# A decoder step on one core: the DRAM scratch of the second projection's right operands, with the column group ahead of the partition

## The reference

```
h = rms_norm(x, norm_g) @ w_in                      # 2048 x 8192
b_gate, c_gate, hx, z = split(h, 4)
u = c_gate * hx
conv = conv3_causal(prev_u, u)
y = (b_gate * conv * silu(z)) @ w_out               # 2048 x 2048
x = x + y
```

## Time and profile before

| what | value |
|---|---|
| median of 3 runs | 2429.08 us (2425.07 to 2432.25) |
| the profiled execution's own time | 2431.18 us |
| its span | 2429.4 us |
| PE busy | 2342.1 us (96%) |
| DVE busy | 1687.6 us (69%) |
| ACT busy | 1240.2 us (51%) |
| DMA | 571.01 MB in 383174 packets, mean 235 GB/s |
| queue q1 (SyncE), share of 16 DMA engines | 55.0% |
| queue q10 (ScalarE), share | 12.1% |
| PE L1085 and L1089 in the chain that ended last | 22% and 11% of the span |
| "DMA left<-in_w_out_a_dram" in the same chain | 2% |
| loads right_a_rounded<-y_right_scratch | x8, 952 KB, 11.1 us to landing |
| loads right_b_rounded<-y_right_scratch | x6, 952 KB, 14.4 us to landing |

### The profile page before, as it was taken

How to read it: one execution, slowest core, us unless ns; L and a number is a source line. 1 busy time by engine, 2 the same in 40 slices (tenths; PEclk the granted TensorE clock), 3 DMA queues, 4 the chain that set the end, 5 groups by cost and what they waited for, 6 DMA issues and landing times.

```text
span 2429.4 us, 49387 instructions
## 1 busy us (share of the span) xinstructions
PE 2342.1 (96%) x20006; PEld 2041.6 (84%) x20006; DVE 1687.6 (69%) x1984; ACT 1240.2 (51%) x2236; POOL 109.0 (4%) x69
## 2 busy tenths in 40 slices
PE   5999999999998999999999999999999989899998
PEld 4999999999998999999998999999999733355554
DVE  6888788878876884555898978787667667533311
ACT  5544444444443446777555477776655346421111
POOL 3000000000000111000000000000000022200000
PEclk9999999999998999999999999999999999999999
DMA  6243444344348666235577777887889899999998
GB/s 198 87 133 105 137 129 124 103 134 130 104 145 314 211 204 220 87 104 183 197 263 252 248 280 242 302 269 267 280 301 321 309 381 422 369 371 383 383 406 302
DMA packets 383174, 571.01 MB, mean 235 GB/s; under 512 B 19513, under 2 KB 304690, under 8 KB 363698
## 3 DMA queue, kind: packets, MB, share of 16 engines
q1 hardware_dynamic: 305858, 461.55, 55.0%
q10 hardware_dynamic: 76960, 106.03, 12.1%
q0 software_dynamic: 128, 0.26, 0.0%
HBM read 508.24 MB, written 59.54 MB: 234 GB/s over the span
## 4 chain that ended last, share of the span: by engine, by line
PE 82%; DVE 6%; DMA 5%; ACT 3%; issue 2%; SPq 0%; ACTq 0%; DVEq 0%
PE psum L1085 22%; PE psum L1738 18%; PE psum L1089 11%; PE psum L1746 8%; PE psum L2444 8%; PE psum L1789 4%; PE psum L2523 4%; DMA left<-in_w_out_a_dram 2%; PE psum L2502 1%; DVE h_keys_turned L1680 1%; PE psum L1754 1%; PE psum L2483 1%; DMA w_raw<-in_w_in_b_dram 1%; ACT w_raw L1501 1%; PE psum L1768 1%
## 5 line engine op out<-in xcount | busy, mean ns | idle before, releaser
L1738 PE MATMUL psum<-x_hi,w_hi 128*128 128x272 f32 x2048 | 434.4, 293 | 4.3 <-DVE x_lo L993 2.9
L1738 PE MATMUL psum<-x_lo,w_hi 128*128 128x272 f32 x2048 | 425.9, 289 | 0.0
L456 ACT ACTIVATE left_rounded<-left 128x1024 fp32r<-128x1024 f32 x280 | 295.1, 1055 | 192.0 <-PE psum L1089 174.5
L1085 PE MATMUL psum<-right_a_rounded,left_rounded 128*128 128x272 f32 x2560 | 352.3, 290 | 8.8 <-DVE right_a_rounded L779 4.6
L771 DVE TENSOR_TENSOR left_rounded<-left,left_rounded 128x1024 fp32r<-128x1024 f32 x280 | 345.5, 1237 | 20.8 <-ACT left_rounded L456 20.4
L1085 PEld LDWEIGHTS psum<-right_a_rounded,left_rounded 128*128 128x128 f32 x2560 | 335.2, 190 | 10.0 <-issue 8.2
L1738 PEld LDWEIGHTS psum<-x_hi,w_hi 128*128 128x128 f32 x2048 | 322.0, 189 | 21.6 <-issue 21.1
L1738 PEld LDWEIGHTS psum<-x_lo,w_hi 128*128 128x128 f32 x2048 | 322.1, 189 | 0.0
L1680 DVE STREAM_TRANSPOSE h_keys_turned<-h_ring 128x1024 f32<-128x1024 f32 x256 | 300.0, 1215 | 19.7 <-PE psum L1789 10.7
L1746 PE MATMUL psum<-x_hi,w_lo 128*128 128x272 f32 x2048 | 286.1, 295 | 0.0
L1746 PEld LDWEIGHTS psum<-x_hi,w_lo 128*128 128x128 f32 x2048 | 265.9, 189 | 8.5 <-issue 4.9
(11 more groups left out here) (253 smaller groups left out, 2738.0 us busy)
## 6 DMA issues: line engine op xcount, KB each, us to landing
h_ring<-in_cache_k_dram SPq DMA_DIRECT2D x256, 512.0 KB, 6.4
ring<-in_cache_v_dram SPq DMA_DIRECT2D x128, 1024.0 KB, 7.9
left<-in_w_in_a_dram SPq DMA_DIRECT2D x128, 512.0 KB, 4.0
w_raw<-in_w_kv_dram SPq DMA_DIRECT2D x16, 2048.0 KB, 12.8
w_raw<-in_w_in_b_dram SPq DMA_DIRECT2D x15, 2048.0 KB, 9.6
left<-in_w_out_a_dram SPq DMA_DIRECT2D x32, 512.0 KB, 5.8
wo_raw<-in_w_out_b_dram SPq DMA_DIRECT2D x32, 512.0 KB, 8.6
ring<-in_w_out_b_dram SPq DMA_DIRECT2D x16, 1024.0 KB, 7.3
```

Source lines behind the costliest of these rows:

```text
L456: act.activation(arena.left_high(q), arena.left(LEFT[mm], n), ACT.Copy).then_inc(hi_ready, 1)
L1085: pe.matmul(to, wh[:, k * P:(k + 1) * P], arena.right(RIGHT[mm], low)[:, k * GT:(k + 1) * GT], start=(mm in OPENS and k == 0 and low == 0) ...
L1738: pe.matmul(psum[n % 2][:, g, 0:GT], m.WH[n % 2][:, k * P:(k + 1) * P], x[:, k * T + g * GT:k * T + (g + 1) * GT], start=(k == 0 and x is ...
```

## The change

The scratch's dimensions are reordered from (piece, operand, partition, group, column) to (piece, operand, group, partition, column). Before, one partition of one operand was 8 groups of 1088 bytes behind each other in DRAM, and the load of the first seven groups read 7616 contiguous bytes for a partition. Now the 128 partitions of one group lie behind each other, and the load reads 7 rows of 1088 bytes for a partition. In the stores only the destination's addresses move: their rows were 1088 bytes, 8704 apart, and are 1088 bytes, 1088 apart, for the partitions of a group. No instruction is added, removed or moved on any engine; the 14 loads have another shape (128x7x272 instead of 128x1904), and the bytes are the same.

```diff
-                        act.dma_start(st.YS.rearrange("l e p i t -> l i p e t")[0, past][:, 0:3, :],
+                        act.dma_start(st.YS.rearrange("l e i p t -> l i p e t")[0, past][:, 0:3, :],
                                       quarters(low_high.bitcast(F32))).then_inc(y_out, 16)
...
                 for low in range(2):
-                    act.dma_start(arena.right(order, low)[:, 0:(EDGE - 1) * GT].bitcast(F32),
-                                  st.YS[low, entry].rearrange("p i t -> p (i t)")[:, 0:(EDGE - 1) * GT]).then_inc(right_in[mm], 16)
+                    act.dma_start(arena.right(order, low)[:, 0:(EDGE - 1) * GT].bitcast(F32).rearrange("p (i t) -> p i t", i=EDGE - 1),
+                                  st.YS[low, entry].rearrange("i p t -> p i t")[:, 0:EDGE - 1, :]).then_inc(right_in[mm], 16)
...
-        st.YS = nc.dram_tensor("y_right_scratch", (2, PRODUCTS, P, EDGE, GT), F32, kind="Internal").ap()
+        st.YS = nc.dram_tensor("y_right_scratch", (2, PRODUCTS, EDGE, P, GT), F32, kind="Internal").ap()
```

More of the change, by code:

```diff
@@ L543, in conv_extras @@
                         act.wait_ge(yh_ready, 2 * past + 2)
-                        act.dma_start(st.YS.rearrange("l e p i t -> l i p e t")[0, past][:, 0:3, :],
+                        act.dma_start(st.YS.rearrange("l e i p t -> l i p e t")[0, past][:, 0:3, :],
                                       quarters(low_high.bitcast(F32))).then_inc(y_out, 16)
-                        act.dma_start(st.YS.rearrange("l e p i t -> l i p e t")[0, past][:, 3:7, :],
+                        act.dma_start(st.YS.rearrange("l e i p t -> l i p e t")[0, past][:, 3:7, :],
                                       quarters(top_high.bitcast(F32))).then_inc(y_out, 16)
@@ L549, in conv_extras @@
                         act.wait_ge(yl_ready, 2 * past + 2)
-                        act.dma_start(st.YS.rearrange("l e p i t -> l i p e t")[1, past][:, 0, :], y4_low[:, 0, :]).then_inc(y_out, 16)
-                        act.dma_start(st.YS.rearrange("l e p i t -> l i p e t")[1, past][:, 1:3, :], y4_low[:, 2:4, :]).then_inc(y_out, 16)
-                        act.dma_start(st.YS.rearrange("l e p i t -> l i p e t")[1, past][:, 3:7, :], quarters(b1_rounded.bitcast(F32))).then_inc(y_out, 16)
+                        act.dma_start(st.YS.rearrange("l e i p t -> l i p e t")[1, past][:, 0, :], y4_low[:, 0, :]).then_inc(y_out, 16)
+                        act.dma_start(st.YS.rearrange("l e i p t -> l i p e t")[1, past][:, 1:3, :], y4_low[:, 2:4, :]).then_inc(y_out, 16)
+                        act.dma_start(st.YS.rearrange("l e i p t -> l i p e t")[1, past][:, 3:7, :], quarters(b1_rounded.bitcast(F32))).then_inc(y_out, 16)
                 if part == 2 and mm == 0:
```

## The result

The changed kernel takes 2438.92 us in the median of 20 runs (2435.29 to 2445.36), the kernel before 2431.11 us in the median of 20 on the same chips. The ratio is 1.0035, 95% interval 1.0028 to 1.0042: 7.8 us slower by the medians, 6.8 to 10.2 by the interval. The forecast was +4.9 us, and 2434.0 us for the median; 2.0 us of the distance to 2438.92 are the median of the kernel before, which was 2429.08 over the 3 runs known then. The profiled execution took 2438.66 us, its span 2436.8, against 2429.4.

The account below looks back on a forecast made before the run. PE, busy 96%, bounds the kernel, with 14.9 us lost in the loads' stretch. Step 33 later, +5.2, less 0.3 for its first product, gives +4.9: 2436.1 profiled, 2434.0 as median (runs' median 2.1 lower), range 2426 to 2441.

Parts of the forecast that it names:

- Turns between the queues: Load and weight queues alternate packets; with 1088-byte rows the weights' q1 gets near 35%, removing both waits for weights.
- The stores at nothing: The 35 stores keep row size and count, only addresses move; covered by over 10 us, priced at nothing.
- The loads' rows at 48 ns: A 1088-byte load row takes the store's 48 ns; the 14 loads' engine work rises from 32.5 to 37.6 us.
- Rival D: Reading 1088-byte rows costs more than writing them: +7.8 to about +11 us, taken as +9, 2438 us; chance 0.14.
- Rival C: 1088-byte rows move at the byte rate of 7616-byte rows, 41.4 ns each: +0.9 us, 2430.0 us; chance 0.07.
- ScalarE held at its issues: Load issues wait until about 1,230 rows are left ahead; last passes at 761.8, (32, 1) starts at 764.3 instead of 753.01.
- Rival B: ScalarE isn't held at the load issues; the DMA engines bound the stretch: -1.6 us, 2427.5 us; chance 0.18.
- What is won back: From (32, 1) on nothing is missing; six products take 18.1 us, step 33 starts at 782.4 instead of 777.19.
- I take nothing, the bound is +2.8: PE's clock after standing some 12 us inside (32, 0): a low clock priced at nothing, at most +2.8 us.
- slower by over 0.3%: Whole kernel over 7.3 us slower: chance 0.22, of it 0.14 dearer reads and 0.08 low clock or poor overlap.
- main case: ScalarE held at the load issues makes the kernel +4.9 us, 2434.0 us, bounds +2.6 to +9.1; chance 0.52.
- within 0.3%: Whole kernel's time within 7.3 us of no change: chance 0.71.

Follow-up runs that it names:

- stores_only: Changed kernel with loads reading 7616 contiguous bytes per partition of the new layout, right operands' values misordered: 2431.46 us, ratio 0.9998 to the kernel before.
- weights_ahead_1088: Changed kernel with loads issued from SyncE, step 33's weights A22 and A11 ahead of the last two right operands: 2430.0 us, ratio 1.0000 to the kernel before.
- weights_ahead_7616: Kernel before with loads issued from SyncE, step 33's weights A22 and A11 ahead of the last two right operands: 2427.58 against 2431.04 us, ratio 0.9986.
- last_first: Changed kernel with two small copies, last_right(0) and last_right(1), moved ahead of the last pair of loads on ScalarE: 2433.8 us, ratio 1.0005 to the kernel before.
- sp_loads_7616: Kernel before with loads issued from SyncE between the weights, step 33's A11 behind the last right operand: 2432.92 against 2430.03 us, ratio 1.0004.
- rows_4_3: Kernel before with operands stored in two halves, each loaded by its own DMA, rows of 4352 and 3264 bytes: 2433.73 against 2430.03 us, ratio 1.0010.
- halved_7616: Kernel before with each load cut into two DMAs of 64 partitions, same 7616-byte rows: 2461.23 against 2431.04 us, ratio 1.0128.

## Why the prediction was right, and where its size was off

- **Turns between the queues:** right. 715 packets against 718, q1 at 39.8% instead of 9.7%; the wait for "left<-in_w_out_a_dram" ahead of (31, 6) is gone. The issues took its place: TensorE waited 5.73 us there, before 4.55.
- **The stores at nothing:** right, by stores_only (ratio 0.9998, 0.9989 to 1.0007).
- **The loads' rows at 48 ns, 44.8 each:** right, 45.0 in the load itself, and one per 46.1 ns from 744 to 747 us. Rival D, dearer reads, needed 48.5 and is out. Rival C, the byte rate of long rows, is out too: it needed a listed 41.4 ns, and the load's rows have 49.4 (1.096 x 48 us / 1066); weights_ahead_1088 is also 2.4 us behind weights_ahead_7616. The Trainium skill ("DMA: Bandwidth & Descriptors", Specifications) says that 512 bytes suffice for full rate. These runs don't agree between 1088 and 7616 bytes.
- **ScalarE held at its issues:** right, and the place of it. `take_u3(31)` at 743.18 (predicted 743.4), (31, 6) at 744.26 (744.5), the last issue accepted at 761.50 (761.8). That the last time fits within 0.3 us is in part luck, since two errors cancel. The level was off, some 1,470 rows instead of 1,230, and fewer rows of weights had gone through (3,876 packets of q1, semaphore writes included, against the 4096 rows of the sum), which together is worth 1.1 us; the engines were some 0.9 us slower than the sum had it. Rival B is out.
- **What is won back:** right. No wait from (32, 1) on.
- **The term that was off: "I take nothing, the bound is +2.8"** for the clock behind the long wait. The 10 matmuls that end (32, 0) took 2.40 us (762.66 to 765.06) instead of 1.34, and (32, 1) 4.52 instead of 3.01: 2.6 us. With them step 33 would start 5.2 + 2.6 = 7.8 us later, against 7.26 in the trace, and the whole is 4.9 + 2.6 = 7.5, against 7.8 by the medians. The prediction says that no row shows whether the clock is low after a wait of 12 us. The nearest row pointed that way: (31, 6) took 4.96 us behind a wait of 4.55, the longest wait there. I left it out of that bound, weighed only the resumptions at 771.62 (slow) and 751.67 (at full speed), and took the one that cost nothing.
- **The chances:** "slower by over 0.3%" had 0.22, since I put the clock in the top of the main case alone. 0.35% lies there, and "within 0.3%", which had 0.71, is missed by a little; the interval (0.28 to 0.42%) reaches into both. The range, 2426 to 2441, holds.

## What to carry to other kernels

A DMA's rows cost twice: the engines' time, and the room in the issuing engine's queue. Before cutting a transfer into more rows, add up the rows that will be ahead of each issue; here holds of several us came from some 1,000 rows on (and two short ones with fewer), and the issuing engine stopped, with all that stood behind the issue. Issue bursts from an engine that has nothing to compute, in the order in which the data is due (weights_ahead_7616), or put the urgent small work ahead of the issue (last_first).

Shorter rows do hand the other queue its share, packet for packet. One ordered queue did that here without more rows, for 0.14% (weights_ahead_7616), and only in the right order: sp_loads_7616 won nothing.

## What the runs showed that I had not expected

- A load to 64 partitions moved its rows at half the rate of one to 128: 0.52 us instead of 0.29 for 7616 bytes, 235 instead of some 420 GB/s, +30 us for the kernel. I haven't shown why.
- Groups of issues on ScalarE's queue were held until some 920 to 980 rows were left ahead (rows_4_3, halved_7616), and until some 1,470 were left in the changed kernel; two single issues were long with fewer. The limit isn't one number of rows and isn't nine DMAs.
- After a wait of 11.74 us TensorE came back at half its clock, after one of 1.90 us at full clock; but in stores_only (32, 1) took 4.53 us after a wait of 2.24 us. The waits of 4.55 us (before), 6.91 (last_first) and 10.83 (rows_4_3) were also followed by slow matmuls. For the short waits the length doesn't settle it, and what does is open.
